# Four more chunk groups in the seven-product stretch of a two-block kernel, and the two parts beside it on half and two thirds of the chunks

## What is computed

```
hn = rmsnorm(h, norm_mix_w[l])
q, k, v, g_ret, xr, yr, g_a, g_b = jnp.split(hn @ w_in[l], offsets, axis=-1)
q = rotary(q...); k = rotary(k...) * (RET_QK_DIM ** -0.5)
ret = head_groupnorm(chunkwise_retention(q, k, v), ret_gn_w[l])
ret_out = jax.nn.silu(g_ret) * ret
xr = causal_dwconv(xr, ...);  hr = rg_lru(xr, ...)
rnn_out = jax.nn.gelu(yr) * hr
merged = sigmoid(g_a) * (ret_out @ w_proj_ret) + sigmoid(g_b) * (rnn_out @ w_proj_rnn)
```

## Time and profile before

| | before |
|---|---|
| median of 3 runs | 3410.67 us (3409.99 to 3411.6) |
| the profiled execution's own time | 3410.22 us |
| its span, first to last instruction | 3408.6 us |
| PE busy | 3388.1 us, 99% |
| DVE busy | 2328.8 us, 68% |
| ACT busy | 1657.3 us, 49% |
| POOL busy | 219.5 us, 6% |
| mean share of the 16 DMA engines, GB/s | 217 GB/s over the span |
| granted TensorE clock | 0.999 |

### The profile page before, as it was taken

One profiled execution on the slowest core, in us unless ns is written; L12 is line 12 of the kernel. 1 busy time (PEld: TensorE's weight loads), 2 busy tenths in 40 slices (PEclk: granted clock), 3 DMA queues, 4 the chain that ended last, 5 costly groups with the idle time before them and its releaser, 6 DMA issues.

```text
span 3408.6 us, 43818 instructions
## 1 busy us (share of the span) xinstructions
PE 3388.1 (99%) x15956; PEld 2770.9 (81%) x15956; DVE 2328.8 (68%) x2835; ACT 1657.3 (49%) x2168; POOL 219.5 (6%) x407
## 2 busy tenths in 40 slices
PE   8999999999999999999999999999999999999999
PEld 6778877778888877888888888888888888888887
DVE  5659977768687657568967674656545687877644
ACT  6442244443354246546655554444454566666443
POOL 1010110101100100100011000000000000000000
PEclk9999999999999999999999999999999999999999
DMA  9978845556867735666777676765654666666665
GB/s 376 399 240 272 281 137 184 180 183 244 272 200 247 274 114 192 239 188 200 236 250 235 203 241 204 251 216 186 206 172 153 189 185 195 187 189 190 203 192 167
DMA packets 331823, 738.86 MB, mean 217 GB/s; under 512 B 26423, under 2 KB 27025, under 8 KB 328448
## 3 DMA queue, kind: packets, MB, share of 16 engines
q1 hardware_dynamic: 298496, 620.83, 57.2%
q0 software_dynamic: 30640, 106.22, 8.7%
q10 hardware_dynamic: 2512, 9.45, 0.8%
HBM read 691.19 MB, written 45.21 MB: 216 GB/s over the span
## 4 chain that ended last, share of the span: by engine, by line
PE 97%; DMA 1%; DVE 1%; ACT 1%; issue 0%; SPq 0%; POOL 0%; ACTq 0%; DVEq 0%; POOLq 0%
PE psum L751 28%; PE psum L753 28%; PE psum L752 28%; PE psum L1327 1%; PE psum L2844 1%; PE psum L2843 1%; PE psum L2842 1%; PE psum L1350 1%; DMA w_raw<-xa_w_k 1%; PE psum L1336 1%; PE psum L1394 1%; PE psum L577 0%; PE psum L2856 0%; PE psum L2857 0%; PE psum L2858 0%; PE psum L2182 0%
## 5 line engine op out<-in xcount | busy, mean ns | idle before, releaser
L648 DVE TENSOR_TENSOR w_lo<-w_raw,w_hi 128x1024 fp32r<-128x1024 f32 x933 | 1139.6, 1224 | 887.9 <-ACT w_hi L640 884.6
L640 ACT ACTIVATE w_hi<-w_raw 128x1024 fp32r<-128x1024 f32 x933 | 984.6, 1059 | 1195.4 <-PE psum L753 1075.1
L751 PE MATMUL psum<-w_hi,a_hi 128*128 128x512 f32 x2816 | 1114.6, 396 | 1.8 <-ACT stage L674 1.1
L753 PE MATMUL psum<-w_hi,a_lo 128*128 128x512 f32 x2816 | 1097.7, 390 | 0.0
L752 PE MATMUL psum<-w_lo,a_hi 128*128 128x512 f32 x2816 | 1096.1, 389 | 0.0
L751 PEld LDWEIGHTS psum<-w_hi,a_hi 128*128 128x128 f32 x2816 | 529.0, 188 | 113.6 <-issue 4.5
L753 PEld LDWEIGHTS psum<-w_hi,a_lo 128*128 128x128 f32 x2816 | 528.6, 188 | 112.0
L752 PEld LDWEIGHTS psum<-w_lo,a_hi 128*128 128x128 f32 x2816 | 529.3, 188 | 105.8
L598 DVE SCALAR_TENSOR_TENSOR ada_sum<-ada_raw,cond_st,ada_sum 128x1024 f32<-128x1024 f32 x240 | 299.8, 1281 | 10.3 <-DMA ada_raw<-w_ada 6.0
L751 PE MATMUL psum<-w_hi,f_hi 128*128 128x512 f32 x704 | 275.0, 391 | 0.0
L753 PE MATMUL psum<-w_hi,f_lo 128*128 128x512 f32 x704 | 274.1, 389 | 0.0
(11 more groups left out here) (445 smaller groups left out, 3490.1 us busy)
## 6 DMA issues: line engine op xcount, KB each, us to landing
w_raw<-w_in SPq DMA_DIRECT2D x416, 512.0 KB, 4.4
ada_raw<-w_ada SPq DMA_DIRECT2D x176, 512.0 KB, 5.9
w_raw<-ffn_w_up SPq DMA_DIRECT2D x176, 512.0 KB, 3.7
w_raw<-w_out SPq DMA_DIRECT2D x96, 512.0 KB, 4.6
w_raw<-ffn_w_down SPq DMA_DIRECT2D x88, 512.0 KB, 4.8
p<-stage POOLq DMA_DIRECT2D x152, 256.0 KB, 4.8
w_raw<-xa_w_k SPq DMA_DIRECT2D x32, 512.0 KB, 10.0
w_raw<-xa_w_v SPq DMA_DIRECT2D x32, 512.0 KB, 8.3
```

Source lines behind the costliest of these rows:

```text
L640: nc.scalar.activation(w_hi[:, slot], raw_of(k), ACT.Copy).then_inc(hi_ready, 1)
L648: nc.vector.tensor_tensor(w_lo[:, slot], raw_of(k), w_hi[:, slot].bitcast(F32), ALU.subtract).then_inc(lo_ready, 1)
L751: nc.tensor.matmul(acc, g.hi[:, tt, kt, :], w_hi[:, slot, kk, :], start=first, stop=False)
L753: mm = nc.tensor.matmul(acc, g.lo[:, tt, kt, :], w_hi[:, slot, kk, :], start=False, stop=last)
```

## The change

g_ret and g_a move in front, into the seven-product stretch, which now has xr, yr, g_ret and g_a: 16 chunks, 8 pairs. The recurrent part runs beside q, k and v alone (8 chunks, 64 pieces) at 1.34 steps a piece, and the retention beside g_b alone (4 chunks, 32 pieces) at 1.08. No step of either part is changed. The load of `decay` now counts on the second `rqk` semaphore, so the rotation of the second tile waits for it as well, and the two later waits are renumbered.

```diff
         parts2 = [Gemm(w2, cols_of(start), n, 2, *act_a, func=func, to=to2(p2), rs=mix_rs) for start, n, func in (
-            (6144, 4, ACT.Copy), (8192, 4, ACT.Gelu_apprx_tanh), (0, 8, ACT.Copy), (10240, 4, ACT.Sigmoid),
-            (4096, 4, ACT.Silu), (12288, 4, ACT.Sigmoid))]
-        rnn_part, qkv_part, ret_gate_part = parts2[1], parts2[2], parts2[4]
+            (6144, 4, ACT.Copy), (8192, 4, ACT.Gelu_apprx_tanh), (4096, 4, ACT.Silu), (10240, 4, ACT.Sigmoid),
+            (0, 8, ACT.Copy), (12288, 4, ACT.Sigmoid))]
+        rnn_part, qkv_part, ret_gate_part = parts2[1], parts2[4], parts2[2]
-        plan["win2"], plan["win2_rnn"], plan["win2_ret"] = parts2[0:2], parts2[2:4], parts2[4:6]
+        plan["win2"], plan["win2_rnn"], plan["win2_ret"] = parts2[0:4], parts2[4:5], parts2[5:6]
...
-            pool.dma_start(decay[:], t["decay"]).then_inc(r_w_loaded, 16)
+            pool.dma_start(decay[:], t["decay"]).then_inc(r_loaded[1], 16)
...
-                dve.wait_ge(r_loaded[tt], 16)
+                dve.wait_ge(r_loaded[tt], 16 + 16 * tt)
...
-                    dve.wait_ge(r_w_loaded, 16)
+                    dve.wait_ge(r_loaded[1], 32)
...
-                    pe.wait_ge(r_w_loaded, 48)
+                    pe.wait_ge(r_w_loaded, 32)
...
-        RNN_RATE, RET_RATE, TURN_RATE, MERGE_RATE = 0.89, 0.54, 0.5, 1.0
+        RNN_RATE, RET_RATE, TURN_RATE, MERGE_RATE = 1.34, 1.08, 0.5, 1.0
```

## The result

| | before | the change |
|---|---|---|
| median | 3410.07 us (7 runs, 3409.89 to 3411.6) | 3422.73 us (7 runs, 3420.78 to 3425.6) |
| ratio | | 1.0036, 95% interval 1.0027 to 1.0045 |
| profiled execution, its span | 3410.22, 3408.6 us | 3425.6, 3423.9 us |

What follows compares the result with a forecast made beforehand. PE, busy 3388.1 of 3408.6 us, bounds the kernel: only fewer matmuls save time, and PE's waits lose it. -8.2 - 0.9 + 8.2 + 11.9 = +11.0 us on 3410.22 gives 3421 us, range 3411 to 3428.

Steps and rivals of the forecast that it cites:

- The 36 matmuls: Seven-product stretch: four more pairs turned over issue 36 matmuls fewer, 8.2 us less, with DVE's 93% load costing nothing.
- The recurrent part: At 1.34 steps a piece, PE waits at the start, reciprocals and quarters' ends: 8.2 us more, between 4 and 11.
- The reciprocal: Recurrent part: PE waits for the split behind DVE's reciprocal, 0.6 us in each of three quarters, 0.8 in the fourth.
- The quarter's end: Recurrent part: PE's transposes wait 1.7 us for a_lo before the second, third and fourth quarter.
- The start: Recurrent part's start: PE waits for the loads of xr, between 0 and 2 us, taken as 0.5.
- -0.9 for the old wait: Recurrent stage: its one earlier wait, where ACT's square root met a chunk's end, disappears, 0.9 us less.
- The retention's start: Store, load and rotation of q and k end at T + 28.2 (T: recurrent part's end); PE waits 11.9 us.
- rival C: Retention's start: while PE stops, no weights load, so store and load are quicker by 4.4 us; 3417 us, chance 0.14.
- rival D: PE's rests lower its clock to 1.2 GHz, or loads delay weights and store: 3 to 7 us more, 3426 us, chance 0.12.
- Decay with q and k costs nothing: Retention: decay, issued with q and k 19 us before the second tile's rotation, arrives in time, so no cost.
- A: Only the retention's start costs; DVE keeps its margins in the recurrent part: +1.5, 3412 us, no change; chance 0.12.
- B: The gain arrives: rotation done before PE has finished six pieces and quarters end in time; 3401 us, chance 0.04.

Runs made afterwards that it cites:

- e5: The change, with PE waiting before a quarter's transposes for L2138's results instead of a_lo; 3420.01 us, 1.0030.
- e4: The change with five empty steps before the retention's steps on PE, ACT and DVE (POOL's 12 become 17), rate 1.13; 3418.8 us, 1.0025.
- e9: The change with q and k loaded by tiles, the first in the recurrent part's last quarter, before v's store is waited for; 3415.88 us, 1.0018.
- e12: The change with q and k by tiles, decay six steps later, first-quarter loads early, second's late, e5's wait and the reciprocal halved; 3412.28 us, 1.0003.
- e13: e12 with decay's load waiting for PE's transposes of the first tile, and xr and yr issued half a set after the gate weights; 3406.54 us, 0.9991.
- e2: Against the kernel before, only g_a moves in front; recurrent part beside q, k, v at 1.34, retention beside g_ret and g_b at 0.54; 3422.27 us, 1.0033.
- e1: Against the kernel before, only g_ret moves in front; recurrent part beside q, k, v, g_a at 0.89, retention beside g_b at 1.08; 3413.6 us, 1.0010.
- e11: e7 with the second quarter's loads also issued ten steps later; 3420.51 us, 1.0031.
- e7: The change with the first quarter's gate weights, xr and yr issued one set of four chunks earlier, in the seven-product stretch; 3423.63 us, 1.0040.

## Why the prediction was right, and where not

- *The 36 matmuls*: -8.2 predicted, -8.1 in the ledger. DVE at 93% for seven pairs cost nothing, as said.
- *The recurrent part*: +8.2 predicted, +11.5 found (the ledger's 10.6 has the old wait's -0.9 in it), half a microsecond outside the bounds of 4 to 11. The reciprocal was 0.55 us a quarter for 0.6 (0.4 for 0.8 in the last). The quarter's end was 1.3 us for 1.7, and e5 shows that it is this wait. The start was the term that was mis-sized: 0.5 said, 3.4 found, and 1.6 more of lower clock behind it. POOL had issued the four loads 7.2 us after the stage's start, as estimated. I took their landing from the earlier trace rows, 6.0 us, but they now run beside the last stores, the second quarter's loads and the weights: PE goes on 9.7 us after the last of the four was issued, and the slowest load of that group lands after 10.8.
- *-0.9 for the old wait*: right, it has no place in the list any more. With it the sum found is -8.1 - 0.9 + 11.5 + 12.5 = +15.0 us, for the +11.0 predicted. That the median lies only 1.7 us above the 3421 is in part luck: the execution that these terms are read from lies 4.4 above it.
- *The retention's start*: +11.9 predicted, +12.5 found. The chain came as written and a microsecond faster: issue T + 10.2 for T + 8.8, the load 5.0 us for 7.5, as rival C had it for the time in which PE and its weights stand still, rotated T + 27.2 for T + 28.2. Against the T + 16.3 at which PE would ask, that is 10.9 us for 11.9; it holds the two waits, 8.7 us of the "about 12" that the prediction named as its sign, and the first burst of slower matmuls (1.8 us), which lies between them and would else have been waited out. The second burst, behind the transposes, comes on top with 1.7 us. So the size was right by two errors of a microsecond or two: a load that was quicker, and a clock that I had given to rival D and to no term.
- *Decay with q and k costs nothing*: wrong in general. In the change itself it costs nothing that its trace shows: ACT waits 2.7 us for w_raw at most, and PE rests in the meantime. As soon as the rest is repaired, its megabyte on top of the others makes ACT wait 5.5 to 5.9 us for weights (e4, e9, e12), and moving it is worth part of the 5.7 us between e12 and e13.
- *Rivals.* A (only the retention's start) fell with the ledger and e2. B fell. C's mechanism was there (2.5 us on the load) and the first half of D's too (1.7 and 1.6 us beside what was waited out), and they nearly cancelled. The clock fell behind rests of 3.2, 6.4 and, right after that one, 1.9 us, and not behind those of 1.2. The Trainium skill ("TensorE: Matmul & The Clock Gate", "Why this matters for your kernels") warns that idle gaps of TensorE take its clock to half. The trace agrees, and adds that a rest of 2.5 us had it in one run (e12, 0.43 us a matmul behind it) and not in another (e9, 0.227). D's other half was there as well: the store was waited for 7.6 us, where the chain before had 5.6.
- C's price by the Trainium skill's formula ("DMA: Bandwidth & Descriptors", "Anatomy of one DMA - SWDGE (gpsimd) path"), 4.4 us for a megabyte, an estimate, came near where PE stood still (5.0 us) and not elsewhere (9.1 us in e1). The same page ("Rules for kernel authors") says that DMAs of several issuing engines run on the same 16 DMA engines and interleave; the trace agrees: ACT waits 5.9 us for w_raw, issued by SP, beside 2 MB of POOL's (e12) and 2.8 beside one (e13).

Two small slips in the prediction's figures change nothing: the lower bound of 4 us for the recurrent part, called the quarters' ends alone, would be 3 x 1.7 = 5.1, and half of C's chance of 0.14 is 0.07, not 0.05.

What stays open: what the last 0.5 us of the recurrent part are, why runs of a kernel in which PE rests scatter over 3 to 6 us (e13's 11 runs over 2.3), and what e12's and e13's two edits are worth apart from each other, which was not tried.

## What to carry to other kernels

Moving a cheap block away from a busy step saves what the block costs, but the block was also the time in which loads landed and results were made. Before such a move, list for each engine the margin with which its results arrive, and subtract. Space large loads by a wait for a result, not by steps, since an engine that only issues has no time of its own; beside two megabytes at once ACT waited 6 us for weights here, beside one at a time 3.

## What was not expected of the hardware

- A rest of PE costs more than its length: 3.5 us at 1.2 GHz behind 8.7 us of waits, of which 1.8 lay within the delay anyway, and 1.6 us behind 3.4.
- The same 1 MB load took 5.0 us from issue to first use while PE stood still (the change), and 9.1 while PE went on (e1). The wait for a store differs as much with its place: 7.6 us at the retention's start, 5.6 in the earlier trace rows.
- Issuing 1.5 MB early is not free in a stretch whose DMA share is 0.69: ACT waited 4.2 to 4.9 us for a weight piece (e11, e12, e7), and PE lost 2 us, half of what it was to save.
